# An expert's bias rows loaded behind its eight gate/linear slabs in place of behind the first four

## What is computed

```python
def expert_block(args):
    xb, e = args
    gu = xb @ w_gu[e] + b_gu[e]
    g, lin = jnp.split(gu, 2, axis=-1)
    g = jnp.minimum(g, SWIGLU_LIMIT)
    lin = jnp.clip(lin, -SWIGLU_LIMIT, SWIGLU_LIMIT)
    act = g * jax.nn.sigmoid(SWIGLU_ALPHA * g) * (lin + 1.0)
    return act @ w_down[e] + b_down[e]
```

## Time and profile before

| what | us |
|---|---|
| time, median of 3 runs | 2062.66 |
| lowest and highest of the 3 | 2062.09, 2065.93 |
| the profiled execution's own time | 2051.78 |
| its span, first to last instruction | 2050.0 |
| PE busy | 1937.4 |
| DVE busy | 993.8 |

### The profile page before, as it was taken

One profiled execution on the slowest core, in us unless ns is written; L12 is line 12 of the kernel. 1 busy time (PEld: TensorE's weight loads), 2 busy tenths in 40 slices (PEclk: granted clock), 3 DMA queues, 4 the chain that ended last, 5 costly groups with the idle time before them and its releaser, 6 DMA issues.

```text
span 2050.0 us, 53441 instructions
## 1 busy us (share of the span) xinstructions
PE 1937.4 (95%) x20292; PEld 801.4 (39%) x20293; DVE 993.8 (48%) x2301; ACT 356.0 (17%) x740; POOL 501.0 (24%) x540
## 2 busy tenths in 40 slices
PE   5999989968999999999999999999999999999996
PEld 3444444533333333334343343334334443334432
DVE  4666546354434435454444454545445454444435
ACT  4143120221110101111111111111111111111003
POOL 1100022132222222323232322323223232322221
PEclk9999999989999999999999999999999999999998
DMA  9233307341771864959596969879797897999995
GB/s 373 84 144 123 123 19 228 124 164 50 281 278 26 331 227 125 396 172 363 183 350 213 393 248 372 300 282 388 284 395 281 306 373 283 388 395 376 318 337 196
DMA packets 125697, 527.37 MB, mean 257 GB/s; under 512 B 17248, under 2 KB 47600, under 8 KB 75472
## 3 DMA queue, kind: packets, MB, share of 16 engines
q1 hardware_dynamic: 92272, 470.46, 59.1%
q0 software_dynamic: 33184, 56.29, 11.9%
q10 hardware_dynamic: 192, 0.06, 0.0%
HBM read 494.35 MB, written 32.38 MB: 257 GB/s over the span
## 4 chain that ended last, share of the span: by engine, by line
PE 80%; DMA 13%; DVE 2%; SPq 1%; ACT 1%; issue 1%; POOL 1%; DVEq 0%; ACTq 0%; POOLq 0%
PE psum L1339 40%; PE psum L1359 21%; PE psum L1081 8%; DMA big<-in_exp_w_gu_dram 7%; PE psum L1255 5%; DMA big<-in_exp_w_down_dram 5%; PE psum L1192 2%; SPq L524 1%; PE psum L1124 1%; PE psum L1299 1%; DMA big<-in_w_in_dram 0%; ACT r L836 0%; DMA big<-in_w_out_dram 0%; PE psum L1311 0%; PE psum L1210 0%
## 5 line engine op out<-in xcount | busy, mean ns | idle before, releaser
L1339 PE MATMUL psum<-big,r 128*32 128x512 f32 x9152 | 1005.2, 597 | 30.6 <-DMA big<-in_exp_w_gu_dram 23.4
L1339 PEld LDWEIGHTS psum<-big,r 128*32 128x32 f32 x9152 | 290.9, 110 | 698.2 <-issue 646.5
L1359 PE MATMUL psum<-big,r 128*32 128x256 f32 x9152 | 511.8, 383 | 17.7 <-DVE r L1984 15.0
L733 POOL DMA_INDIRECT acc_rows<-r,scatter_idx x139 | 220.4, 1586 | 779.7 <-DVE r L1994 749.5
L1359 PEld LDWEIGHTS psum<-big,r 128*32 128x32 f32 x9152 | 294.8, 111 | 214.0 <-DVE r L1984 15.3
L964 ACT ACTIVATE r<-r,shift 128x128 f32<-128x128 f32 x368 | 150.9, 481 | 884.7 <-PE psum L1339 828.0
L1969 DVE TENSOR_TENSOR r<-psum,r 128x256 f32<-128x256 f32 x143 | 60.6, 424 | 339.8 <-PE psum L1339 337.0
L722 POOL DMA_INDIRECT r<-hs_rows,gather_idx x188 | 184.9, 983 | 83.8 <-issue 41.2
L1991 DVE TENSOR_TENSOR r<-psum,r 128x256 f32<-128x256 f32 x143 | 60.7, 425 | 273.2 <-PE psum L1359 272.2
L1081 PE MATMUL psum<-r,big 128*128 128x512 f32 x384 | 168.1, 598 | 2.1 <-DMA big<-in_w_in_dram 2.1
L1942 DVE STREAM_TRANSPOSE r<-r 128x1024 f32<-128x1024 f32 x46 | 95.8, 2082 | 106.0 <-issue 106.0
(11 more groups left out here) (316 smaller groups left out, 937.0 us busy)
## 6 DMA issues: line engine op xcount, KB each, us to landing
big<-in_exp_w_gu_dram SPq DMA_DIRECT2D x256, 1024.0 KB, 12.0
big<-in_exp_w_down_dram SPq DMA_DIRECT2D x128, 1024.0 KB, 21.3
big<-in_ada_w_dram SPq DMA_DIRECT2D x12, 2048.0 KB, 13.8
r<-in_x_dram SPq DMA_DIRECT2D x16, 512.0 KB, 9.7
big<-in_w_in_dram SPq DMA_DIRECT2D x4, 2048.0 KB, 19.8
r<-in_exp_b_gu_dram SPq DMA_DIRECT2D x128, 64.0 KB
big<-in_w_out_dram SPq DMA_DIRECT2D x2, 2048.0 KB, 12.8
hs_rows<-r POOLq DMA_DIRECT2D x8, 512.0 KB, 3.0
```

What stands on the lines that cost most here:

```text
L733: pool.indirect_dma_start(acc_quarters, bass.IndirectOffsetOnAxis(ap=scatter_idx[:, u:u + 1], axis=0), y_sb[:, u, :], None, bounds_check=4 ...
L1339: last = pe.matmul(psum[32 * j:32 * j + 32, u, :].rearrange("p (a n) -> p a n", a=2), izT[:, k, u * UNIT:(u + 1) * UNIT], rhs[:, :, 256 * ...
L1359: ins_ = pe.matmul(psum[32 * i:32 * i + 32, 4 + u % 2 if bank is None else bank, 0:256], actT[:, u, f, :], down_slab(f)[:, 256 * i:256 * i ...
```

## The change

In the load loop over the places 1 to 31 the block with the two waits and the eight bias DMAs is taken when q is 7 in place of 3. The load of place 0 (ahead of the loop) is as it was. Nothing else differs, and no instruction is added or removed.

```diff
                 for q in range(CHUNKS):
                     sp_.wait_ge(freed[q], done)
                     load_chunk(e, q)
-                    if q == 3:
+                    if q == 7:
 
                         sp_.wait_ge(bias_in, SEMW * 8 * place)
                         if place >= 2:
```

## The result

| | runs | median us | lowest and highest |
|---|---|---|---|
| kernel before | 6 | 2062.38 | 2060.05, 2065.93 |
| changed kernel | 6 | 2048.76 | 2047.97, 2050.95 |

The ratio is 0.9939, with a 95% interval of 0.9928 to 0.9950. The changed kernel is 13.6 us faster; the forecast was 1.7 us, and its range ended at 2056.0 us.

A forecast was written before the change was run, and what follows sets the result against it. It took matmuls held up by slab transfers as the bound. Gains of 0.94 and 0.76 us, all else 0, made 2062.66 - 1.70 = 2061.0 us, own range 2059 to 2063.5, 8-in-10 range 2056.0 to 2067.0 us.

The forecast's parts named there:

- What bounds the kernel: Whole kernel: matmuls held up by transfers in places; in places 16 to 24 chunk 11's landing sets the end.
- Gain of the five: 0: Places 16 to 24: chunk 11 lands as before, so time won at chunk 7 is lost there; gain 0.
- The first rival: Down slabs come earlier too, so all seven chunk 7 waits shrink: 9.6 us gained, 2053.0 us; chance 0.12.
- chunks 0 to 3 of even places: Waits there, such as 2.33 us in place 12, were taken as unchanged, having the same bytes ahead in either order.
- The price of a set: Queue time of one expert's eight bias DMAs: 1.5 us, between 1.02 us by bytes and 2.08 us.
- Chunk 7 shrinks by up to 1.5 us: Places 16 to 24: waits of 1.40 to 2.01 us at chunk 7 shrink by up to 1.5 us.
- Places 12 and 14, 1.70 us: Waits at chunk 7 there have room before chunk 11: 0.94 and 0.76 us gained, sum 1.70 us.
- the second rival: Clock falls at the new chunk 11 waits in five places: 6.8 us slower, 2069.5 us; chance 0.11.
- SP's issuing, cost 0: SP's 3.5 us of bias waits and issues move between chunk 7 and freed4's successor freed8; nothing seen, cost 0.
- bias rows in time, cost 0: Bias rows still reach DVE in time: up to 2.2 us later is free in place 18; cost 0.
- The rule to issue early: Skill's rule to issue transfers early would leave the bias rows in place; the prediction followed the trace instead.
- The base: Timed median lies 10.88 us above the profiled execution; this was added unchanged to the forecast.

The follow-up runs named there:

- the second trace of the changed kernel: The changed kernel, unaltered, profiled and timed again: 2046.06 us, ratio 0.9916 to the kernel before.
- the second trace of before: The kernel before, unchanged, profiled a second time, span 2059.4 us; timed at 2061.74 us, ratio 0.9988.
- The tiny DMAs: Changed kernel plus eight DMAs of 32 x 4 bytes per expert: behind chunk 3 2097.78 us, behind chunk 7 2081.18 us; with only one, behind chunk 3, 2050.15 us.
- the three DMAs: Bias set loaded by three DMAs in place of eight, same bytes: in the changed kernel, behind chunk 7, 2113.21 us; in the kernel before, behind chunk 3, 2153.53 us.

## Why the prediction was wrong

*What bounds the kernel* held: waits for transfers, and the run of two places up to the landing of chunk 11 as what sets the pair's length. With no bias rows the time falls by 33.8 us.

*"Chunk 11 has the same slabs and bias rows in front of it as before, so it lands when it did ... Gain of the five: 0."* This step failed. The bytes in front of chunk 11 are the same, but the time that they take depends on the order: a set costs 2.1 to 2.3 us behind chunk 3 and 1.5 to 1.75 behind chunk 7, by the landing of chunk 11 in the traces with and without bias rows. Two sets lie in each run, so chunk 11 lands 1.1 us earlier (1.6 in the second trace of the changed kernel), and the period of the pair shrinks by 1.04 us (1.50), which is kept. The five pairs put at 0 are 5.2 us (7.5) of the gain. The first rival had the condition, that the down slabs come earlier too, and its test, a shrinking distance from place to place, came true; it gave no reason for it and put 9.6 us on it in all. The measured 13.6 us lie beyond that, because places 4 and 12, below, gain more than either had for them.

*"In the queue these lie ... behind the whole load of the place before, whose bytes are the same in either order"*, with which I set aside chunks 0 to 3 of even places, failed in the same way: their last now lands 1.4 to 1.7 us earlier. In place 12 the wait at the chunks 0 to 3, 2.33 us ahead of x96 in the earlier trace rows and 1.54 in the second trace of before, became 0.29 and 0.59. Place 4 with such waits gained 2.0 us, a part of it by a shorter clock fall. A share of this is told by the odd places, which have no set ahead of their own chunk 3 in the run: as a mean over six it lands 14.1 and 14.3 us behind the first issue with the bias rows directly behind it (the two traces of before), and 13.4 to 13.6 without (both of the changed kernel and the one without bias rows). So a set also delays the slab in front of it.

*The price of a set*, 1.5 us between 1.02 and 2.08, was a term of the old place, and there it is 2.1 in the trace that I had and 2.3 in the second, at and above my upper bound. I had built both bounds from bytes and rates. The tiny DMAs show that eight DMAs can cost as much with no bytes to speak of.

*Chunk 7 shrinks by up to 1.5 us* was mis-sized: it is 2 to 3.5 us in the table, the place's own set of 2.1 to 2.3 and the rest from the set of the place before. So every wait at the x72 rows went in places 16 to 24 in the first trace, where I left 0.1 to 0.5 us in some; with the stops of the second trace of before two of the five were small or gone already.

*Places 12 and 14, 1.70 us*: 3.1 and 0.5 us, against the second trace of before; against the trace that the forecast was built on it is 1.15 and 1.17, forecast 0.94 and 0.76. In the timed-like trace the wait at chunk 7 of place 12 comes with a clock fall of 6.8 us. The change shortens the wait from 2.57 to 1.79 us without a fall (1.95 with one of 3.4 us in the second trace), and waits for down slabs come in, as forecast. This is the second rival the other way round: I priced a fall that could come, and not one that could go. In place 14 a fall stayed in the first trace.

*The clock between 1300 and 1800 us* is 1.00 before and after; the second rival did not occur; the wait at chunk 11 is at most 1.37 us in one piece there. Its bound, between 2.01 and 2.33 us, does not hold, though. In the second trace of before the clock stays at 1.00 behind 2.11 us in place 20. In the second trace of the changed kernel the wait at chunk 7 of place 12 is 1.95 us, and the granted clock falls behind it, where it had stayed up behind 2.01 us in place 20:

```profile
1162.74 10.51 PE L1339 MATMUL psum<-big,r 128*32 128x512 f32 x96 [0.59 <-DMA big<-in_exp_w_gu_dram]
1175.19 3.33 PE L1339 MATMUL psum<-big,r 128*32 128x512 f32 x20 [1.95 <-DMA big<-in_exp_w_gu_dram]
```

```profile
1176.40:1179.80 3.40, 3.40 (x20) 0.85 (x16) 1.15 (x4) 0.16 (x1) 0.00 (x0) 0.50 1.01 390
```

Twelve us before it there was another wait, of 0.59 us; the length of one wait alone does not tell, and what does is open.

*SP's issuing, cost 0*, and *bias rows in time, cost 0*, held at chunk 7. DVE's addition is put down once to a bias DMA in the changed kernel:

```profile
868.94 0.42 DVE L1969 TENSOR_TENSOR r<-psum,r 128x256 f32<-128x256 f32 x1 [10.98 <-DMA r<-in_exp_b_down_dram]
```

PE goes over to the down products at 878.09 us without idle time there, so nothing is lost. One chunk later both margins are gone: SP's issuing stands between chunks 8 and 9 in a queue that has run empty. I had found slack of 2.2 us in place 18 and 21 us behind a one-unit item, but had not looked at places 1 to 12, where in some the down slabs are released late and a set in front of them delays them.

*The rule to issue early*, which spoke against the change, did not decide here: the Trainium skill, page "DMA: Bandwidth & Descriptors", section "Rules for kernel authors", wants a transfer issued early and waited for late, and the kernel is 13.6 us faster with these eight issued later. The runs with the rows behind chunks 8 and 11 show where lateness begins to cost.

*The base*: I took over the 10.88 us between trace and median "as it is". Had I asked what was different in the timed runs, the trace could not have told; the second trace shows short stops in two-unit items (11 us, the same with the change) and in places 4 and 12 longer clock falls, from which the change takes more.

*A slip in the sum*: the bias rows would land "1.0 to 2.1 us behind the new chunk 7" of 1442.0, that is 1443.0 to 1444.1; the 1443.5 is the middle. Nothing rests on it.

What stays open: why a set of eight is 0.35 to 0.8 us dearer behind chunk 3. A packet of 1 KB took 69 ns there and 55 ns behind chunk 7 (mean over the 4608 of them from 1290 to 1800 us in the second trace of each; 70 and 58 in the first), which is 24 x 0.014 = 0.34 us a set on each engine. That is about half of it, and the tiny DMAs, with no such packets, show 0.5 us too, while the three DMAs show nothing.

Of all versions run the changed kernel is the fastest that computes the reference.

## What to carry to other kernels

Do not price small DMAs in a queue of large ones by their bytes; how they spread over the engines counts, and eight cost more than one. Take the price from two traces with and without them rather than from a rate. "The same transfers stand in front of it" does not mean "it lands at the same time". Where the profiled execution is not like the timed runs, take a second profile before making a sum of waits of one to three us.

## What the runs showed of the hardware

- Eight DMAs of 128 bytes each lengthened a run of slabs by 1.9 us behind chunk 7 and by 2.4 us behind chunk 3; in a stretch of 3 us in which they passed, the DMA engines were busy 0.40 of the time though slabs were queued behind them.
- Eight DMAs of 384 KB in all cost 2.1 to 2.3 us behind the fourth slab and 1.5 to 1.75 us behind the eighth, and the slab directly in front of them landed 0.5 to 1.0 us later with them behind it.
- A DMA whose outermost dimension is 4 used four of the 16 engines: four of the sixteen landing events of chunk 11 came 2.6 to 4.3 us behind the other twelve, and three such DMAs of 128 KB cost 5.5 to 5.7 us.
- The granted clock fell to 0.50 for 6.8 us in and behind a wait of 2.57 us, and for 3.4 us behind one of 1.95 us, but not behind waits of 2.01 and 2.11 us.
- Two executions of the same kernel differed by 9.4 us in span, with stops of about 1 us in eleven items of the one and none in the other.
